# Moving the sums of squares between blocks from GpSimd to VectorE, and moving weight roundings and low parts by one unit

## What is computed

```python
for layer in range(DEPTH):
    m = mixer_ab(rmsnorm(x, g[0]), ...) if layer % 2 == 0 else mixer_cd(rmsnorm(x, g[0]), ...)
    x = x + rmsnorm(m, g[1])
    x = x + rmsnorm(cross_attn(rmsnorm(x, g[2]), mem, ...), g[3])
    x = x + rmsnorm(sq_relu_mlp(rmsnorm(x, g[4]), ...), g[5])

def rmsnorm(x, g):
    y = x * lax.rsqrt(jnp.mean(x * x, axis=-1, keepdims=True) + RMS_EPS)
    return y * g
```

## Time and profile before

| | |
|---|---|
| time, median of 3 runs | 960.18 us (957.38 to 960.84) |
| the profiled execution | 955.97 us, span 954.1 us |
| TensorE busy | 895.4 us, 94% |
| VectorE busy | 671.7 us, 70% |
| ScalarE busy | 471.2 us, 49% |
| GpSimd busy | 194.6 us, 20% |
| transfers | 153.73 MB, mean 161 GB/s |

### The profile page before, as it was taken

How to read it: one execution, slowest core, us unless ns; L and a number is a source line. 1 busy time by engine, 2 the same in 40 slices (tenths; PEclk the granted TensorE clock), 3 DMA queues, 4 the chain that set the end, 5 groups by cost and what they waited for, 6 DMA issues and landing times.

```text
span 954.1 us, 17154 instructions
## 1 busy us (share of the span) xinstructions
PE 895.4 (94%) x7268; PEld 869.6 (91%) x7268; DVE 671.7 (70%) x1058; ACT 471.2 (49%) x661; POOL 194.6 (20%) x167
## 2 busy tenths in 40 slices
PE   6999998999989999999889998999999799999997
PEld 6899988888979999999789988899988799999996
DVE  5897996786396555554969999966686485555553
ACT  5545544565465444445543433636474454445443
POOL 1000800120021000000348778447120030000000
PEclk9999999999999999999999999999999899999999
DMA  8454434534545655655545654244542445665651
GB/s 289 135 177 135 151 111 149 183 112 145 167 151 181 195 185 192 189 187 177 177 132 179 198 156 139 84 152 156 177 134 89 133 136 195 198 191 188 195 179 45
DMA packets 81030, 153.73 MB, mean 161 GB/s; under 512 B 6251, under 2 KB 7227, under 8 KB 80955
## 3 DMA queue, kind: packets, MB, share of 16 engines
q1 hardware_dynamic: 80843, 152.60, 50.2%
q10 hardware_dynamic: 112, 0.05, 0.0%
HBM read 151.58 MB, written 1.05 MB: 160 GB/s over the span
## 4 chain that ended last, share of the span: by engine, by line
PE 57%; DVE 34%; ACT 4%; issue 2%; POOL 2%; DMA 1%; DVEq 0%; POOLq 0%
PE ps L495 18%; PE ps L497 18%; PE ps L496 18%; DVE w_lo L1274 9%; DVE ps L1641 7%; DVE h_lo L1285 3%; ACT w_hi L921 2%; DVE tmp L1579 1%; DVE E L1445 1%; DVE xT L1586 1%; DVE xc L1346 1%; POOL w_lo L1914 1%; DVE cv L1804 1%; DVE E L1453 1%; PE ps L562 1%
## 5 line engine op out<-in xcount | busy, mean ns | idle before, releaser
L921 ACT ACTIVATE w_hi<-raw 128x1024 fp32r<-128x1024 f32 x284 | 295.5, 1054 | 233.6 <-DMA raw<-in_mlp_w 131.6
L495 PE MATMUL ps<-h_hi,w_hi 128*128 128x256 f32 x1280 | 360.5, 282 | 33.8 <-DVE w_lo L1274 21.3
L1274 DVE TENSOR_TENSOR w_lo<-raw,w_hi 128x1024 fp32r<-128x1024 f32 x238 | 294.3, 1258 | 127.7 <-ACT w_hi L921 122.8
L497 PE MATMUL ps<-h_hi,w_lo 128*128 128x256 f32 x1280 | 356.7, 279 | 0.0
L496 PE MATMUL ps<-h_lo,w_hi 128*128 128x256 f32 x1280 | 356.7, 279 | 0.0
L495 PEld LDWEIGHTS ps<-h_hi,w_hi 128*128 128x128 f32 x1280 | 242.7, 190 | 39.5 <-DVE w_lo L1274 25.4
L496 PEld LDWEIGHTS ps<-h_lo,w_hi 128*128 128x128 f32 x1280 | 243.0, 190 | 0.1
L497 PEld LDWEIGHTS ps<-h_hi,w_lo 128*128 128x128 f32 x1280 | 242.6, 190 | 0.0
L497 PE MATMUL ps<-r_hi,w_lo 128*128 128x256 f32 x512 | 144.4, 282 | 0.0
L495 PE MATMUL ps<-r_hi,w_hi 128*128 128x256 f32 x512 | 144.3, 282 | 0.0
L496 PE MATMUL ps<-r_lo,w_hi 128*128 128x256 f32 x512 | 144.3, 282 | 0.0
(11 more groups left out here) (247 smaller groups left out, 1275.7 us busy)
## 6 DMA issues: line engine op xcount, KB each, us to landing
raw<-in_mlp_w SPq DMA_DIRECT2D x128, 512.0 KB, 3.9
raw<-in_cd_w_in SPq DMA_DIRECT2D x40, 512.0 KB, 3.7
raw<-in_xa_wkv SPq DMA_DIRECT2D x32, 512.0 KB, 4.0
raw<-in_ab_w_in SPq DMA_DIRECT2D x24, 512.0 KB, 4.4
raw<-in_xa_wq SPq DMA_DIRECT2D x16, 512.0 KB, 3.9
raw<-in_xa_wo SPq DMA_DIRECT2D x16, 512.0 KB, 3.9
raw<-in_cd_w_out SPq DMA_DIRECT2D x16, 512.0 KB, 3.7
raw<-in_ab_w_out SPq DMA_DIRECT2D x12, 512.0 KB, 3.8
```

What stands on the lines that cost most here:

```text
L495: nc.tensor.matmul(dst, wt[0], x[0], start=start, stop=False, skip_group_check=True)
L497: return nc.tensor.matmul(dst, wt[1], x[0], start=False, stop=stop, skip_group_check=True)
L921: nc.scalar.activation(w_hi[:, v % SLOTS, :, :], raw[:, v % SLOTS, :, :], ACT.Copy)\
L1274: V.tensor_tensor(w_lo[:, v % SLOTS, :, :], raw[:, v % SLOTS, :, :], f(w_hi[:, v % SLOTS, :, :]), ALU.subtract).then_inc(lo_ready_dve, 1)
```

## The change

The sums of the squares of the new x are made by VectorE instead of GpSimd: the first of them inside `new_x` behind the low part of tile 4, the others behind the low part of the unit N+4. TensorE and ScalarE wait for VectorE's count instead of GpSimd's. ScalarE rounds one unit further at each place of a boundary: N+1 before `Nrow` where there is a filler, and N+2 to N+5 inside `new_h`. VectorE makes the low part of N+1 before `new_x` (at (1,1) before the norm's sums), that of N+2 behind tile 3, of N+3 behind tile 6; before, those of N+1, N+2 and N+3 stood behind tiles 3, 5 and 7.

```diff
@@ TensorE, three places (tags in1, q0/q1, mlp0/mlp1)
-                pe.wait_ge(pool_made, after("pool", "Sx", f"q{l}"))
+                pe.wait_ge(dve_made, after("dve", "Sx", f"q{l}"))
                 token_sums(("astat", l), halves(S2))
@@ ScalarE, new_h
                             if i >= 2:
-                                act.wait_ge(pool_made, after("pool", "Sx", tag, 0 if i == 2 else 1))
+                                act.wait_ge(dve_made, after("dve", "Sx", tag, 0))
                             nc.scalar.activation(sq[:, i % 2, :].rearrange("p (c t) -> p c t", c=2),
                                                  xT[:, j - 1:j + 1, :], ACT.Square)\
                                 .then_inc(act_made, tick("act", "xsq", tag, i))
-                            round_to(base + i + 1)
-                    round_to(base + 5)
+                            round_to(base + i + 2)
@@ ScalarE, boundary
                     if fill:
-                        round_to(nxt)
+                        round_to(nxt + 1)
@@ VectorE
+            def x_sums(tag):
+
+                for i in (2, 3):
+                    dve.wait_ge(act_made, after("act", "xsq", tag, i))
+                    own()
+                    V.tensor_tensor(Ssum[:, :], Ssum[:, :], sq[:, i % 2, :], ALU.add).then_inc(dve_made, tick("dve"))
+                own()
+                V.tensor_tensor(S2[:, :], Ssum[:, 0:T], Ssum[:, T:H2], ALU.add).then_inc(dve_made, tick("dve", "Sx", tag))
+
@@ VectorE, new_x
                         low_h(tag, gl, gs, j - 2)
-                        if j % 2 == 1:
-                            low_to(lows[j // 2 - 1])
+                        low_to(lows.get(j - 2, -1))
+                        if j == 6:
+                            dve.wait_ge(act_made, after("act", "xsq", tag, 1))
+                            V.tensor_tensor(Ssum[:, :], sq[:, 0, :], sq[:, 1, :], ALU.add)\
+                                .then_inc(dve_made, tick("dve", "Sx", tag, 0))
@@ VectorE, boundary
-                low_to(x)
+                low_to(x if fill else x + 1)
                 norm_sum(l, n, m)
...
                 dve.wait_ge(pool_made, after("pool", "nr", l, n))
-                low_to(nxt if fill else nxt + 1)
-                new_x(l, n, m, tag, gl, gs, [nxt, nxt + 1, nxt + 2, nxt + 3])
-                if tag:
-                    low_to(nxt + 4)
+                low_to(nxt + 1)
+                new_x(l, n, m, tag, gl, gs, {3: nxt + 2, 6: nxt + 3})
+                low_to(nxt + 4)
+                x_sums(tag)
@@ GpSimd: x_sums and its three calls go
-                pool.wait_ge(act_made, after("act", "xsq", tag, 1))
-                G.tensor_tensor(Ssum[:, :], sq[:, 0, :], sq[:, 1, :], ALU.add).then_inc(pool_made, tick("pool", "Sx", tag, 0))
...
-                G.tensor_tensor(S2[:, :], Ssum[:, 0:T], Ssum[:, T:H2], ALU.add).then_inc(pool_made, tick("pool", "Sx", tag))
```

More of the change, by code:

```diff
@@ L785, in _ @@
                         if n == 0:
-                            pe.wait_ge(pool_made, after("pool", "Sx", "in1"))
+                            pe.wait_ge(dve_made, after("dve", "Sx", "in1"))
                             token_sums(("xstat", 0), halves(S2))
@@ L886, in _ @@
                 w1(0)
-                pe.wait_ge(pool_made, after("pool", "Sx", f"mlp{l}"))
+                pe.wait_ge(dve_made, after("dve", "Sx", f"mlp{l}"))
                 token_sums(("hstat", l), halves(S2))
@@ L1974, in _ @@
             low_to(F_[("V", 0, 0)] - 1)
-            def x_sums(tag):
-                pool.wait_ge(act_made, after("act", "xsq", tag, 1))
-                G.tensor_tensor(Ssum[:, :], sq[:, 0, :], sq[:, 1, :], ALU.add).then_inc(pool_made, tick("pool", "Sx", tag, 0))
-                L.also("pool", "Sx", tag, 1)
-                for i in (2, 3):
-                    pool.wait_ge(act_made, after("act", "xsq", tag, i))
-                    own()
-                    G.tensor_tensor(Ssum[:, :], Ssum[:, :], sq[:, i % 2, :], ALU.add).then_inc(pool_made, tick("pool"))
-                own()
-                G.tensor_tensor(S2[:, :], Ssum[:, 0:T], Ssum[:, T:H2], ALU.add).then_inc(pool_made, tick("pool", "Sx", tag))
             for l in range(2):
@@ L2014, in _ @@
                 low_to(F_[("q", l, 0)] + 3)
-                x_sums(f"q{l}")
                 pool.wait_ge(dve_made, after("dve", "av", l))
@@ L2023, in _ @@
                 low_to(F_[("w1", l, 0)] + 3)
-                x_sums(f"mlp{l}")
                 pool.wait_ge(dve_made, after("dve", "hv", l))
@@ L2041, in _ @@
                     low_to(F_[("gate", 0)] + 3)
-                    x_sums("in1")
     return L.at
```

## The result

The kernel after the change takes 944.85 us in the median of 6 runs (941.4 to 947.05), the kernel before 959.53 in 6 runs beside it (956.29 to 960.84): ratio 0.985, 95% interval 0.983 to 0.987, so 14.7 us less. The forecast was 950.3, its range 945.5 to 956.0: faster, as said, but by 0.65 us outside the range. The two profiled executions are only 10.4 us apart, 955.97 and 945.4 us of time, spans of 954.1 and 943.7. There the forecast had been 9.9. So the first question is where the gain of 10.4 comes from, and the second why the medians lie further apart.

A forecast was written before the change was run, and what follows sets the result against it. VectorE sets TensorE's pace at a boundary, and GpSimd slows VectorE. Terms 2.65 + 2.0 + 2.9 + 0.4 + 1.9 = 9.9 us take the profiled 955.97 to 946.1, the median 960.18 to 950.3; range 945.5 to 956.

The forecast's parts named there:

- (1,1): Boundary without filler: TensorE no longer waits for N+3, 2.1 us less 0.15 for S2, so 1.9 us won.
- (0,0): Boundary where TensorE no longer waits for N+1 and N+2, and N+3 ends earlier: 2.65 us won and kept.
- (0,2): Boundary where 3.7 us are won by the end of N+3, 2.9 left at the factor's matmuls.
- (1,0): Boundary before layer 1's attention: 0.4 of 2.7 us kept, since VectorE's list up to the first maxima is hardly earlier.
- Low part of N+1 ahead of `new_x`: VectorE's first `tmp` moves 1.14 us back, hidden by the filler: 0.7 us to spare at (0,0), none at (0,2).
- Tiles 4 and 5 for at most 0.6: At (0,2) TensorE waits for these two tiles for at most 0.6 us together.
- The rounding ahead of `Nrow`: ScalarE's third rounding, 1.05 us, fits its idle time before `Nrow`: cost nothing, bounds 0 and 1.05 us a boundary.
- rival D: A rounding waits for N+1's late transfer and holds up `Nrow` and `new_x`: median 959 to 961; chance 0.06.
- The new wait for S2: At (0,1) and (0,2) TensorE asks for S2 right after N+3 and waits for VectorE: 0.6 us lost.
- Rival B: Gain given back further on, through VectorE's list in layer 0 or its full stretch: median 953.0 or 955.9; chance 0.19.
- I take it that the clock stays at 2.4 GHz there: At (0,2) the half-clock stretch goes: 1.2 of the 3.7 us won there.
- rival C: Half clock at (0,2) stays (1.2 us), waits in layer 1's attention bring another stretch (2): median 953.5; chance 0.10.

## Why the prediction came close and where it was wrong

*The mechanism held.* GpSimd's sums slowed VectorE's `h_lo`, idle adds of the same kind do it again and cost TensorE 2.9 us at one boundary, and with the sums on VectorE alone the whole gain is there. The placement, which alone brings 8 us, adds nothing to it that can be seen.

*The terms of the sum*, in the two profiled executions, whose clocks are nearly alike (0.989 and 0.988):

| place | forecast, us | measured, us | from |
|---|---|---|---|
| (0,0) | 2.65 | 2.77 | N to the sums, 17.85 to 15.08 |
| (0,1) | 2.0 | 2.25 | the same, 15.17 to 12.92 |
| (0,2) | 2.9 | 3.3 | N to the factor, 18.87 to 15.56 |
| (1,0) with the attention behind it | 0.4 | -0.8 | N to the sums, 17.56 to 14.79; to the norm's sums of (1,1), 48.58 to 52.12 |
| (1,1) | 1.9 | 1.9 | N to the sums, 15.14 to 13.23 |
| all | 9.9 | 10.4 | the spans, 954.1 to 943.7 |

The five places add up to 9.5. Of what is outside them, 1.5 us is a half-clock stretch at 630 us that the first execution of before has and after has not (from the factor to the next sums 10.71 against 9.19 us); the start of the kernel, 0.5 us later in after, stands against it.

*The steps.* "Low part of N+1 ahead of `new_x`" held: at (0,0) TensorE starts N at 185.13 and doesn't pause for N+1. "Tiles 4 and 5 for at most 0.6" at (0,2) was 0.26. The rounding ahead of `Nrow` cost nothing that can be seen, and rival D is out: S, 181.96, is 1.65 behind its old place, of which the low part of N+1 explains 1.14 and the start of the boundary, 0.5 later with TensorE's N (185.13 against 184.62), the rest. The new wait for S2, 0.6, was 0.30 and 0.38. Rival B is out as well: what (0,0) and (0,2) win is still there, to 0.2 us, 58 and 145 us later. At (1,0) the new pause at the transposes came as described; without the half-clock stretch the place keeps 0.9 of the 2.8.

*Two steps about the clock failed.* "I take it that the clock stays at 2.4 GHz there" at (0,2): a half-clock stretch stands at 477.5 to 481.5, and one more at 716.5 in layer 1's attention. That is rival C as it was written. It did not lower the gain between the two traces, because the first execution of before has as many: the prediction says "the full clock elsewhere" of its trace, but that has a stretch at 630 us too, and between 100 and 900 us both executions lose the same, 6.9 and 6.8 us. So the 1.2 us of clock inside the 9.9 did not come.

*Part of the match of 9.9 and 10.4 is luck.* Over the whole span before lost 10.5 us of clock (0.011 x 954) and after 11.3 (0.012 x 944). Without that the gain is 11.2, where the pauses stood in the sum at 8.7 (9.9 less the 1.2). Most of the 2.5 is at (0,2), where TensorE wins 3.2 us up to the sums at 621.44 us with as much clock lost on either side, against 1.7, and 0.5 at (1,0).

The step that put the time outside the range is the last one of the sum: "The profiled execution goes from 955.97 to 946.1. It was 4.2 us below the median (960.18); on that median the forecast is 950.3." The distance to the median was carried over as if it belonged to both kernels. It belongs to before: its profiled execution stands 3.6 us below its median (955.97, 959.53), after's 0.55 above (945.4, 944.85), and the two make the 4.1 us between 10.6 (the two times; the spans give 10.4) and 14.7. A second execution of before had the same pauses and 15.3 us of lost clock between 100 and 900 us where it had 6.9 (of these 8.4 the first one takes 1.7 back by a stretch at 12 us that the second doesn't have, which leaves the 6.7 between them). So the missing term is what the clock costs before, and no longer after, over many executions. Its size by the granted clock: 0.9857 (21 runs) against 0.989 is 0.0033 x 958 = 3.2 us; another group of before had 0.987 (23 runs), and gives 1.9. Filling before's pauses without shortening anything gave 2.2 (0.5 to 4.2). The term was set at 1.2 and is 2 to 4. Between 2 and 4 the runs don't decide, since the gain itself is known only to 12.5 to 16.4 us.

The forecast of 950.3 is 5.4 us above the 944.85. Of these, 0.65 is the median of before (960.18 against 959.53), 2.5 the pauses, and the 2.3 left are, by subtraction, the clock's, whose term is then 3.5 instead of 1.2, within the 2 to 4.

The Trainium skill's "TensorE: Matmul & The Clock Gate", section "HAM oscillation", says that a loop whose work is shorter than its waits is throttled anew at each one. No stretch here is such a loop: the pauses ahead of N+3, 3.10 us at most, stand alone between units of 2.8 us of work each, and still the half clock came at all four of them in the profiled execution, and behind before's shorter ones at (0,0) in one execution and not in the other. The prediction applied the rule to the waits moved into the attention, and a stretch did come there, at 716.5 us. But it stands behind a pause of 2.35 us that the kernel before has too (2.31), without a stretch, and those waits stand alone as well. So no run here tests the rule.

The Trainium skill's "Perfetto Trace Analysis", section "Optimizing Scalar/DVE Operations", says that work of a saturated VectorE may go to ScalarE or even GpSimd. The prediction took that as a rule against the change. But the same passage goes on that GpSimd and VectorE share a read port of SBUF, so that moving work between those two might not help, and the runs agree with that: taking it back won 14 us, and VectorE with the sums is busy 665.2 us, without them 671.7.

## What to carry to other kernels

Ask what a helper engine's instruction reads before counting it as free: work on GpSimd that reads SBUF can cost VectorE more than doing it itself. A short pause of TensorE can cost clock on top of its length, in some executions only. So profile the kernel before more than once before pricing a change from its half-clock stretches, and give the clock a term and a spread of its own. When two traces agree with a forecast, compare their lost clock before calling it right.

## What was not expected of the hardware

- Two executions of one kernel with the same pauses differ by 6.6 us in time (955.97 and 962.54), through the granted clock alone (0.989 and 0.982: 0.007 x 958 = 6.7).
- One unit's low part 2.2 us later at four places cost 15.8 us of time, of which the granted clock explains 7.4 and longer pauses 4.4.
- At a granted clock of 1.00 the matmuls of layer 0's MLP took 170.6 us in one kernel and 173.7 in another, with no pause above 0.4 us: they follow one another at about 0.114 or about 0.118 us, and no run tells why.
- Beside GpSimd's reads, VectorE's `h_lo`, which reads two tensors from SBUF, goes from 0.48 to 1.52 us (two operands read on GpSimd) or 0.83 (one). Beside VectorE's low part of a weight it is the GpSimd add of 512 columns that gets longer: it takes 1.40 us in one place and 2.23 (4.46 for two) there.
- Unread matmuls in the pause at (0,0) cost nothing and kept the clock up (5.57 against 7.18 us behind it), and over the kernel they still bring back less in the median than the mean clock promises (3.4 of 6 us).
